# Attention loads regrouped by column block and head pair, and constants waited for later

## The reference, cut to what matters

```python
h = rms_norm(x, norm1_g) * (1 + scale1) + shift1
z = h @ w_in
q, k, v, ca, cg = jnp.split(z, [...], axis=-1)
...
s = jnp.einsum('bqhd,brqchd->bhqrc', q_r, k_win) * scale + bias[None]
p = jax.nn.softmax(s...)
out = jnp.einsum('bhqrc,brqchd->bqhd', p, v_win)
...
x = x + gate1 * (jnp.concatenate([attn_out, conv_out], axis=-1) @ w_out)
x = x + gate2 * expert_choice_ffn(h2, w_router, w_gate, w_up, w_down)
```

## Time and profile before

| | |
|---|---|
| time, median of 3 runs | 3413.82 us (3413.45 to 3413.94) |
| profiled execution, its own time | 3411.49 us |
| its span, first to last instruction | 3409.3 us |
| mean granted TensorE clock | 0.965 |
| PE busy | 93% |
| DVE, ACT busy | 67%, 56% |
| `front` | 0 to 499 us |
| `attend` | 499.7 to 656 us |

### The profile page before, as it was taken

How to read it: one execution, slowest core, us unless ns; L and a number is a source line. 1 busy time by engine, 2 the same in 40 slices (tenths; PEclk the granted TensorE clock), 3 DMA queues, 4 the chain that set the end, 5 groups by cost and what they waited for, 6 DMA issues and landing times.

```text
span 3409.3 us, 50511 instructions
## 1 busy us (share of the span) xinstructions
PE 3169.9 (93%) x18950; PEld 2832.9 (83%) x18950; DVE 2298.9 (67%) x3457; ACT 1911.0 (56%) x3096; POOL 150.8 (4%) x209
## 2 busy tenths in 40 slices
PE   5999877798099999999999999999999999999997
PEld 3777654587089999999999999999999999999997
DVE  4678815633757776767677776767677676767675
ACT  5143435655056666666666665666666666666654
POOL 0000000000000100101010010101010010101000
PEclk8999988999589999999999999999999999999999
DMA  8321137232345766657575765757576665757572
GB/s 308 130 62 53 47 100 248 104 131 93 146 178 218 264 231 241 241 201 275 193 288 218 251 237 226 254 206 277 194 273 226 241 250 221 263 187 278 210 253 87
DMA packets 136261, 690.67 MB, mean 203 GB/s; under 512 B 12032, under 2 KB 39824, under 8 KB 112528
## 3 DMA queue, kind: packets, MB, share of 16 engines
q1 hardware_dynamic: 125824, 659.68, 51.9%
q0 software_dynamic: 7168, 25.17, 3.2%
q10 hardware_dynamic: 3088, 3.10, 0.3%
HBM read 650.14 MB, written 37.77 MB: 202 GB/s over the span
## 4 chain that ended last, share of the span: by engine, by line
PE 72%; DVE 2%; DMA 0%; POOL 0%; ACT 0%; issue 0%; POOLq 0%; DVEq 0%
PE psG L1318 32%; PE psG L1320 15%; PE psY L1334 5%; PE psY L1337 5%; PE psY L1335 5%; PE psY L1336 5%; PE psY L1338 5%; DVE idxu L1508 1%; DVE affT L1510 1%; DVE vals L1506 1%; PE psG L1285 0%; PE psG L1286 0%; DMA xg_s<-xhat_d,inow 0%; ACT xst L1417 0%; DVE xe L1529 0%
## 5 line engine op out<-in xcount | busy, mean ns | idle before, releaser
L1318 PE MATMUL psG<-xe,w_gu_hi_part 128*128 128x384 f32 x5632 | 1630.8, 360 | 4.2 <-DVE xe L1529 4.2
L1320 PE MATMUL psG<-xe,w_gu_lo_part 128*128 128x192 f32 x5632 | 1411.3, 251 | 0.0
L1320 PEld LDWEIGHTS psG<-xe,w_gu_lo_part 128*128 128x128 f32 x5632 | 1076.9, 191 | 7.9
L1318 PEld LDWEIGHTS psG<-xe,w_gu_hi_part 128*128 128x128 f32 x5632 | 1058.9, 188 | 12.6 <-DVE xe L1529 4.6
L1519 DVE TENSOR_TENSOR w_gu_lo_part<-raw_gu,w_gu_hi_part 128x1024 fp32r<-128x1024 f32 x704 | 858.8, 1222 | 117.8 <-ACT w_gu_hi_part L1428 117.8
L1428 ACT ACTIVATE w_gu_hi_part<-raw_gu 128x1024 fp32r<-128x1024 f32 x704 | 741.2, 1055 | 13.1 <-DMA raw_gu<-in_w_gu 13.1
L1553 DVE TENSOR_TENSOR gu<-psG,low 128x384 f32<-128x384 f32 x352 | 195.7, 556 | 569.3 <-ACT low L1458 569.3
L1524 DVE TENSOR_TENSOR w_dn_lo_part<-raw_dn,w_dn_hi_part 128x1024 fp32r<-128x1024 f32 x352 | 431.0, 1224 | 0.5 <-ACT w_dn_hi_part L1439 0.5
L1458 ACT ACTIVATE low<-psG 128x384 f32<-128x384 f32 x352 | 172.0, 489 | 417.0 <-PE psG L1320 417.0
L1439 ACT ACTIVATE w_dn_hi_part<-raw_dn 128x1024 fp32r<-128x1024 f32 x352 | 367.7, 1045 | 0.8 <-PE psY L1338 0.8
L1417 ACT ACTIVATE xst<-psG,modv,a 128x128 f32<-128x128 f32 (+1 forms) x256 | 95.7, 425 | 392.2 <-PE psG L1320 325.4
(11 more groups left out here) (161 smaller groups left out, 3185.3 us busy)
## 6 DMA issues: line engine op xcount, KB each, us to landing
raw_gu<-in_w_gu SPq DMA_DIRECT2D x176, 2048.0 KB, 7.9
raw_dn<-in_w_down SPq DMA_DIRECT2D x176, 1024.0 KB, 8.8
shared<-in_ada_w SPq DMA_DIRECT2D x12, 2048.0 KB, 9.7
bias<-in_bias SPq DMA_DIRECT2D x8, 1536.0 KB, 12.3
w_raw<-in_w_in SPq DMA_DIRECT2D x20, 512.0 KB, 5.6
qk_d<-shared SPq DMA_DIRECT2D x8, 768.0 KB, 3.8
qk<-qk_d SPq DMA_DIRECT2D x8, 768.0 KB, 11.5
out<-wo_raw SPq DMA_DIRECT2D x12, 512.0 KB, 2.6
```

Of the source, the lines that this page charges most:

```text
L1318: pe.matmul(bank[:, 0:2 * CAP], wh, xe[:, k, :, :].rearrange("p a b -> p (a b)"), start=(k == 0), stop=False, skip_group_check=True)
L1320: mm = pe.matmul(bank[:, 0:CAP], wl, xe[:, k, 0, :], start=False, stop=(k == KD - 1), skip_group_check=True)
```

## The change

- `load_v(eng, j)` now loads a column block j of all six row groups, in 4 transfers of 32 partitions by 6 by 2 KB (384 KB), 16 in all, and all of them on ScalarE's queue. A product of the first four pairs waits for its column block.
- SyncE loads, behind q and k of heads 0 and 1, first the part of the two biases that the prompt's blocks use (columns 0 to 255 of each of three patterns, a semaphore of its own), then the rest of them. VectorE waits for the first part ahead of pair 0 and for the rest ahead of pair 4.
- The other heads follow by pairs: q and k, then their two biases.
- In `front`, ident is loaded by SyncE behind x tile 0 and counts on `c_loaded`. TensorE's first wait and ScalarE's are for that; VectorE's wait for the constants and the scaling of `qkg` move behind its x tile 5; TensorE waits for the constants ahead of its first side matmul.

```diff
@@ front, sync
                 load_x(0)
+                sp.dma_start(ident[:, :], A["ident"]).then_inc(c_loaded, 16)
                 load_x(1)
@@ front, tensor
                     else:
+                        pe.wait_ge(consts, CONSTS)
                         pe.wait_ge(ada_row, MODS)
...
-                pe.wait_ge(consts, CONSTS)
+                pe.wait_ge(c_loaded, 48)
                 turn_x(0)
@@ front, scalar
-                act.dma_start(ident[:, :], A["ident"]).then_inc(consts, 16)
...
-                act.wait_ge(c_loaded, 32)
+                act.wait_ge(c_loaded, 48)
@@ front, vector
-                dve.wait_ge(consts, CONSTS)
-                dve.tensor_scalar(qkg[:, 0:1], qkg[:, 0:1], DH ** -0.5, None, ALU.mult).then_inc(qkg_ready, 1)
                 for t in range(TILES):
...
                     if t == 5:
+                        dve.wait_ge(consts, CONSTS)
+                        dve.tensor_scalar(qkg[:, 0:1], qkg[:, 0:1], DH ** -0.5, None, ALU.mult).then_inc(qkg_ready, 1)
                         ada_rows(0)
@@ attend
-        def load_v(eng, n):
-
-            t0, r0 = V_ROWS[n]
-            for j in range(COL_BLOCKS):
-                for r in range(4):
-                    at = t0 + (r0 + r) * GRID_W + KEY_COL0[j]
-                    eng.dma_start(v[r * K_COLS:(r + 1) * K_COLS, n * COL_BLOCKS + j, :],
-                                  v_d[at:at + K_COLS, :]).then_inc(v_loaded[n], 16)
+        v_rows = v_d.rearrange("(n r c) d -> r c n d", r=4, c=GRID_W)
+
+        def load_v(eng, j):
+
+            for r in range(4):
+                eng.dma_start(v[r * K_COLS:(r + 1) * K_COLS, :, :].rearrange("p (n j) d -> p n j d", j=COL_BLOCKS)[:, :, j, :],
+                              v_rows[r, KEY_COL0[j]:KEY_COL0[j] + K_COLS]).then_inc(v_loaded[j], 16)
@@ attend, sync
                 heads(0)
-                biases(0)
-                biases(1)
-                for n in range(2, len(V_ROWS)):
-                    load_v(sp, n)
+                for h in range(2):
+                    sp.dma_start(bias[:, h, :, 0:256], A["bias"][h][:, :, 0:256]).then_inc(bias_prompt, 16)
+                for h in range(2):
+                    sp.dma_start(bias[:, h, :, 256:BIAS_COLS], A["bias"][h][:, :, 256:BIAS_COLS]).then_inc(bias_loaded[h], 16)
                 for t in range(1, 4):
                     heads(t)
-                for h in range(2, HEADS):
-                    biases(h)
+                    biases(2 * t)
+                    biases(2 * t + 1)
@@ attend, tensor
-                    if h == 0 and j == 0:
-                        for m in range(rows // 4):
-                            pe.wait_ge(v_loaded[first + m], 16 * 4 * COL_BLOCKS)
+                    if u < COL_BLOCKS:
+                        pe.wait_ge(v_loaded[j], 16 * 4)
@@ attend, vector
-                        if b == 0:
+                        if u == 0:
+                            dve.wait_ge(bias_prompt, 32)
+                        if b == 0 and h > 0 or u == COL_BLOCKS:
                             dve.wait_ge(bias_loaded[h % 4], 16 * (h // 4 + 1))
@@ attend, scalar
-                load_v(act, 0)
-                load_v(act, 1)
+                for j in range(COL_BLOCKS):
+                    load_v(act, j)
```

More of the change, by code:

```diff
@@ L262, in front @@
         w_v = A["w_in"].rearrange("(k p) n -> p k n", k=KD)
-        CONSTS = 16 * (5 + CG)
+        CONSTS = 16 * (4 + CG)
         def rows_at(m):
@@ L786, in attend @@
     qk_loaded = [sem(f"qk_loaded{i}") for i in range(4)]
-    v_loaded = [sem(f"v_loaded{i}") for i in range(len(V_ROWS))]
+    v_loaded = [sem(f"v_loaded{i}") for i in range(COL_BLOCKS)]
     bias_loaded = [sem(f"bias_loaded{i}") for i in range(4)]
+    bias_prompt = sem("bias_prompt_loaded")
     s_done, s_biased, p_ready, p_scaled = (
```

## The result

The changed kernel takes 3424.66 us (median of 7, 3423.57 to 3427.78) against 3413.45 us for the kernel before (median of 7 beside it, 3411.15 to 3413.94): ratio 1.0036, 95% interval 1.0024 to 1.0048, so 11.2 us slower. The profiled execution took 3424.03 us where that of before took 3411.49, and its span is 3421.8 us: 12.5 us more by either.

A forecast was written before the change was run, and what follows sets the result against it. Byte arrival was taken to bound `front` from 22 us and attention's first 60 us, a steady pace the rest. Start -4.2 and late v +13.0 gave +8.8 us on 3413.8, so 3422.6; range 3410 to 3431.

The forecast's parts named there:

- The start: In `front`: first normalised tile 9.7 us earlier, but only 4.2 us saved, bounds 3 and 4.5.
- The hole in the DMA stream: In `front`, 15 to 22 us: 1.01 MB moved in 7 us would take 2.5 at 400 GB/s, so 4.5 us.
- The small constant packets: In `front`: constants' packets between 15 and 22 us keep some of the 4.5 us, so 4.2 is taken.
- The sum: In attention: start and mixing, SyncE's 11.01 MB, 1 KB surcharge, v and 2.0 us make 55.8; v there at 555.5.
- v itself: In attention: v's 6.29 MB take 22.7 us, a little under the 23.7 at the rate of before.
- the half-rate rival: Attention: transfers into one quarter of the partitions run at half rate, v 30.8 us, time 3430.7; chance 0.15.
- ScalarE's issues: In attention: v's issues on ScalarE fall from 32 (15.58 us) to 16, about 8 us, done before anything there is needed.
- From the fourth product to the last: In attention: 112.2 us instead of 115.8, so attention ends as before if v lands at 542.5.
- the restart at the low clock: In attention, behind the wait for v: products restart at a low clock, costing 2.4 us once more.
- Wide rate for v (408): Attention: large v transfers run like other loads, v 15.4 us, landing at 547.0, time 3414.1; chance 0.20.
- Bytes shared evenly: Attention: queues share by bytes, not packets; v lands at about 539.5, time 3406.6; chance 0.10.
- The start alone: Only the start counts and v is not late; within or near the first rival (3414.1); chance 0.05.

The follow-up runs named there:

- e3: The changed kernel with SyncE waiting until all of v is there before issuing q, k and biases of heads 2 and later; 3407.66 us, 0.9984 against the kernel before.
- e1: The kernel before with only the `front` part of the change (ident on SyncE's queue, constants waited for later); 3408.14 us, 0.9984.
- e10: The changed kernel with v's 16 transfers on SyncE's queue, behind all biases of heads 0 and 1, ahead of later heads; ScalarE issues none; 3409.55 us, 0.9989.
- e4: As the changed kernel with later loads held until v is in, but v split by partition halves over ScalarE's and SyncE's queues; 3411.08 us, 0.9993.

## Why the prediction was right, and where it was not

**Sign and size.** 3422.6 was forecast, 3424.7 measured. The mechanism holds step by step: the packets of the two queues take turns (157 to 155), v comes behind everything SyncE has issued, the fourth product waits for the last of it, and e3 takes 17 us away by undoing just that. That the total is only 2.1 us off is in part luck: v cost 8.1 us more than its term (30.8 for 22.7), and six smaller differences, named below, took 6.0 back.

**The start.** Forecast 4.2 us with bounds of 3 and 4.5, measured 4.95 in the profile and 5.1 in e1, so a little outside the bounds. The hole in the DMA stream (4.5 us) was the right measure, not VectorE's 10 us. The small constant packets did not keep a part of it, as the forecast had it; where the last 0.45 us come from is open.

**When v lands: the term that was mis-sized.** The sum said 55.8 us from the first load to the fourth product; it was 62.6. The term is v itself, 22.7 us in the sum at a rate a little above the 266 GB/s of before, and 30.5 at the 206 GB/s of e10. I expected larger transfers to run slightly better, for their fewer semaphore updates. The runs showed the opposite: transfers of 384 KB into one block of 32 partitions run at 199 to 207 GB/s, 192 KB in turn at 234, two queues in different halves at 363. With 30.8 for v the sum would have been 63.9. That was the half-rate rival, held at 0.15; the mechanism it names is the one that occurred, and its time (3430.7) was missed by 6.0 us: v came 1.3 us sooner than its sum, the start gave 0.75 more, the way from the fourth product to the last was 0.8 shorter, 1.5 came back in `mix`, 1.3 lie between the profiled execution (+12.5) and the medians (+11.2), and 0.35 between the two medians of the kernel before. The Trainium skill, SBUF — State Buffer, section "Door 1: The DMA port swizzle", gives about 218 GB/s for 32 partitions; the trace agrees within 6% (206 in e10).

**ScalarE's issues.** "About 8 us, and done before anything there is needed" was wrong: 30.77 us, and the first exp at 526.85 where I had it between 513 and 518. It was charged at nothing, and e3 and e10 show that this price was right all the same, as v came later still. In a kernel in which v came earlier it need not be free; no run shows its price there. SyncE too was slower than "all issued by about 508 us": its last of those issues ends at 515.77, still long before v was in, so the sum does not change.

**From the fourth product to the last.** Forecast 112.2 us, measured 111.4; the stall at heads 2 and 3 is gone (products 4 to 13 take 24.54 us, 28.98 before) and the restart at the low clock is there (0.50 in 552:555). Attention ends as before if v lands 42.8 us after the first load; it landed 20 us behind that.

**The rivals.** Wide rate for v (408): with one queue under way the 384 KB transfers never ran above 208. Bytes shared evenly: v had 0.32 of 2.05 MB in 536:542. (Its 539.5 was also added up short: 499.7 + 3.5 + 36 + 2.0 is 541.2.) The start alone: e1 is 5.1 us faster than the kernel before, the changed kernel 11.2 slower.

## What to carry to other kernels

Before transfers are merged and moved to another queue, count what else will then stand beside them. In the kernel before, the sample's v stood on SyncE's queue ahead of the later loads; on the other queue it went in turns with 6.3 MB of them. The prediction put this down to issue time that had acted as a brake. e10 shows that the place is enough: there the later loads are issued while v is still under way and stay behind it. When one consumer needs the last byte of a set, put the set on the queue in the order of need, hold back what is not needed yet, and let transfers of different partition halves be under way at the same time. A faster start is worth the hole that it closes in the DMA stream, not the idle time of the engine that shows it.

## What the hardware showed beyond that

- The DMA engines can read as full (share 1.06 to 1.08) at 199 to 207 GB/s, when 384 KB transfers into 32 partitions each follow one another on one queue; wide loads of the same 2 KB packets moved 408 GB/s at 1.04. A share over 1 does not need two queues, as the section on the time before has it: ScalarE's queue alone has 106.6% in 552:555.
- Issuing a DMA is not a fixed price. The row of v's issues in the changed kernel (min/median/max ns) shows it: single issues took from 0.35 to 5.4 us. In e4 ScalarE issued 8 such transfers in 5.40 us, and in e10 SyncE took 25.45 us for 16 with no other queue beside it. The row does not say what the long ones wait for:

```profile
L818 ACTq DMA_DIRECT2D v<-v_d x16: 353/1138/5416, 494.8 to 520.1; - x16
```
